# Attention probabilities of 16 heads turned in 32-blocks on VectorE and through a DRAM scratch, on one Trainium2 core

## The chip, the cores and the metric

One Trainium2 (trn2) chip, one core of it. The metric is the device time of one launch in microseconds (us). The profile's names: PE is TensorE (PEld its weight loads), DVE is VectorE, ACT is ScalarE, POOL is GpSimd, SP is SyncE; PEq, ACTq and so on are their sequencers. L979 is line 979 of the kernel before.

## The reference

Two blocks of two layers each on a sequence of 256 tokens, D = 1024, float32. The first: a short convolution mixer, then causal attention of 16 heads of 64 (as 256 keys are two of its blocks, each query sees its own block up to itself and all of the block before), each followed by a gated convolution FFN of 2816. The second: a pooling and state-space mixer, then a mixer of 8 heads with a forgetting bias (fox) and 8 latent heads (MLA, 96 wide), each followed by a gated FFN. What the change touches is this, for each head:

```python
sc = jnp.einsum('bhqd,bhkd->bhqk', qi, k).astype(F32) * scale
if fi is not None:
    sc = sc + fi[..., :, None] - log_decay_cum[:, :, None, :]
sc = jnp.where(kpos[None, :] <= qpos[:, None], sc, -jnp.inf)
p = jax.nn.softmax(sc, axis=-1).astype(v.dtype)
return jnp.einsum('bhqk,bhkd->bhqd', p, v)
```

## The kernel before

Everything stays in SBUF; only weights stream in, as 201 chunks of up to 1 MB (`PLAN`). SP loads a chunk into one of 4 raw buffers (`load`, L2153), ACT casts it to its high part (`hi`, L1223), DVE subtracts to get the low part (`lo`, L1570), and PE makes each product as three passes (high times high, high times low, low times high) of fp32r matmuls (`t_part`, L979, for products with tokens in rows; `f_block`, L901 to L923, for products with features in rows).

The order of work is written out by hand. `STEPS` is one list of steps for the whole kernel; each engine's program walks through it and does its own share of each step, in order, with semaphore waits (`Seq.wait_ge`). So a step's place matters only against the other steps of the same engine. The attention stages are the texts `MOBA` (heads 0 to 15) and `ODD` (heads 16 to 31: fox 16 to 23, MLA 24 to 31). In them:

- `tK.T` is a projection step: weight rows K, tokens T. `fN.B` is a step of the other form. `+h` and `+l` are one high cast (and, before, one load) and one low part.
- `sH`: PE makes the scores of heads H and H+1 (in `ODD` of H alone; `scores`, L1020); DVE scales, masks and takes the maxima (`maxima`, L1729); ACT takes the exponentials (`exps`, L1293 and L1295).
- `nH`: DVE multiplies by the reciprocal sum (`normalise`, L1737 to L1740).
- `uH`: PE turns the 128 x 384 probabilities of a head (tokens 0 to 127 against 128 keys, tokens 128 to 255 against 256 keys) in three 128 x 128 transposes into PSUM bank 6 (`turn_probs`, L1030), and ACT copies them out (`copy_probs`, L1302).
- `pH`: PE multiplies the values with the turned probabilities of up to four heads that end with H (`values`, L1048); ACT casts the result to its high part (`heads_hi`, L1306), DVE makes the low part (`split`, L1684).
- `ropeX.Q.T`: DVE rotates queries (Q = 1) or keys (Q = 0) of half X and tokens T (`rope_half`, L1748 to L1754). `crossX.Q.I`: PE turns them for the scores, waiting for both ropes of that half and kind (`cross`, L1058), and ACT copies them out (`copy_cross`, L1313 and L1315). The projection banks of a later stage are free only when the ropes of an earlier one are done (`t_bank_free`).
- In `ODD`, `qcopy` and `kcopy` (L1458, L1459) are ACT's copies of the fox queries and keys; `queriesT` is ACT's copy (L1433) and DVE's rope of the MLA queries; `acrossA.I` turns MLA queries and keys (L1156, copied at L1450) and waits for both `queries`; `kvsT` copies MLA keys and values. Turned probabilities, `cross` and `across` share PSUM bank 6.

A head's probabilities lie in one of four buffers (head number modulo 4), its turned ones in another four. The forget rows of the fox heads go through two small DMAs of SP (`fcrows`), in order with the weight loads.

## Time and profile before

| | us |
|---|---|
| median of 3 runs | 1202.39 (1202.03 to 1202.56) |
| the profiled execution | 1202.26 |
| its span, first to last instruction | 1201.0 |

Busy time in that span: PE 1192.8 us, DVE 880.8, ACT 660.9, POOL 52.6; the DMA engines move 217.8 MB. The granted TensorE clock is 0.999 of its full 2.4 GHz.

How to read it: a timeline row gives the start from the span's first instruction, the duration, engine, line, operation, what is written and read, the shape, and xN where N instructions are merged; in brackets stands the engine's idle time before it and what ended it. Matmuls are pipelined: the duration of one is longer than its distance to the next start, so a group's cost on PE is read from start to start. A `...q` row is the sequencer's, at which the engine itself may be idle.

### The profile page before, as it was taken

What the parts mean: (1) busy time and instruction counts of PE and PEld (TensorE: products, weight loads), DVE (VectorE), ACT (ScalarE), POOL (GpSimd) and SP (SyncE); (2) the same over time, 40 slices, a digit from 0 to 9 for tenths busy, and PEclk for the clock granted to TensorE, in tenths of its full rate; (3) what the DMA queues carried; (4) which work ended last, traced back from release to release, by engine and by line L of the source; (5) the groups of instructions that cost most, each with busy time, mean ns of one, the idle gap of its engine ahead of it and who ended that gap; (6) DMA issues with size and microseconds to landing.
All of it is one profiled execution on the core that took longest, in us unless ns stands there. A gap on an engine that the chain in (4) does not pass through costs nothing.

```text
span 1201.0 us, 16583 instructions
## 1 busy us (share of the span) xinstructions
PE 1192.8 (99%) x6629; PEld 1028.5 (86%) x6629; DVE 880.8 (73%) x1230; ACT 660.9 (55%) x871; POOL 52.6 (4%) x75
## 2 busy tenths in 40 slices
PE   9999999999999999999999999999999999999997
PEld 8888888888877888888899888888889977888886
DVE  6977989846786798883688877776467667777744
ACT  6555666634566666663587645444337775544430
POOL 0000000000000000000005200000002001000000
PEclk9999999999999999999999999999999999999999
DMA  9755555564534455556434556555526433755530
GB/s 357 249 207 192 170 183 188 189 223 162 204 109 141 190 179 177 206 196 218 158 106 141 181 211 240 189 197 188 183 91 229 176 140 106 251 204 176 193 123 35
DMA packets 32653, 217.81 MB, mean 181 GB/s; under 512 B 3760, under 2 KB 4032, under 8 KB 8000
## 3 DMA queue, kind: packets, MB, share of 16 engines
q1 hardware_dynamic: 30704, 210.39, 49.9%
q0 software_dynamic: 1728, 6.29, 1.6%
q8 instruction: 53, 0.87, 0.3%
q14 instruction: 24, 0.20, 0.0%
q10 hardware_dynamic: 144, 0.07, 0.0%
HBM read 215.67 MB, written 1.05 MB: 180 GB/s over the span
## 4 chain that ended last, share of the span: by engine, by line
PE 99%; DVE 0%; DMA 0%; ACT 0%; issue 0%
PE ps L979 43%; PE ps L901 24%; PE ps L907 14%; PE ps L909 4%; PE ps L923 2%; PE ps L920 2%; PE ps L919 2%; PE ps L1020 1%; PE ps L993 1%; PE ps L1048 1%; PE ps L1030 1%; PE ps L1112 1%; DMA t<-in_cst 0%; PE ps L1058 0%; PE ps L934 0%; PE ps L1097 0%
## 5 line engine op out<-in xcount | busy, mean ns | idle before, releaser
L979 PE MATMUL ps<-t,t 128*128 128x512 f32 (+4 forms) x2346 | 536.5, 385 | 0.0
L1570 DVE TENSOR_TENSOR t<-t,t 128x2048 fp32r<-128x2048 f32 (+3 forms) x200 | 448.7, 2256 | 101.4 <-PE ps L979 87.8
L979 PEld LDWEIGHTS ps<-t,t 128*128 128x128 f32 x2346 | 424.8, 188 | 81.4 <-issue 1.8
L1223 ACT CAST t<-t 128x2048 fp32r<-128x2048 f32 (+3 forms) x200 | 374.5, 1882 | 202.3 <-PE ps L979 105.6
L901 PE MATMUL ps<-t,t 128*128 128x512 f32 x1274 | 305.8, 390 | 0.0
L901 PEld LDWEIGHTS ps<-t,t 128*128 128x128 f32 x1274 | 238.9, 188 | 51.2
L907 PEld LDWEIGHTS ps<-t,t 128*128 128x128 f32 x1456 | 187.2, 191 | 7.4
L907 PE MATMUL ps<-t,t 128*128 128x256 f32 x1456 | 189.5, 283 | 0.0
L1719 DVE TENSOR_REDUCE t<-ps 128x512 f32<-128x1024 f32 x40 | 49.0, 1225 | 44.4 <-PE ps L909 44.4
L1672 DVE SCALAR_TENSOR_TENSOR t<-t,t,t 128x254 f32<-128x254 f32 (+1 forms) x176 | 73.2, 478 | 10.2 <-ACT t L1248 10.2
L1288 ACT CAST t<-t 128x512 fp32r<-128x512 f32 x44 | 27.2, 619 | 91.1 <-DVE t L1703 91.1
L1684 DVE TENSOR_TENSOR t<-t,t 128x512 fp32r<-128x512 f32 x48 | 33.2, 692 | 34.9 <-ACT t L1288 32.2
L909 PE MATMUL ps<-t,t 128*128 128x512 f32 x182 | 58.1, 397 | 0.0
L2055 POOL TENSOR_TENSOR t<-t,t 128x1 f32<-128x1 f32 x22 | 15.0, 681 | 935.4 <-DVE t L1625 522.5
L919 PE MATMUL ps<-t,t 128*128 128x256 f32 x192 | 49.0, 288 | 0.0
L920 PE MATMUL ps<-t,t 128*128 128x256 f32 x192 | 48.0, 283 | 0.0
L1284 ACT ACTIVATE t<-t 128x512 f32<-128x512 f32 x42 | 26.4, 628 | 29.2 <-DVE t L1672 29.2
L1248 ACT ACTIVATE t<-t,t 128x256 f32<-128x256 f32 x88 | 39.8, 500 | 1.4 <-DVE t L1999 1.4
L920 PEld LDWEIGHTS ps<-t,t 128*128 128x128 f32 x192 | 36.8, 191 | 0.5 <-issue 0.2
L919 PEld LDWEIGHTS ps<-t,t 128*128 128x128 f32 x192 | 36.7, 191 | 0.5 <-issue 0.2
L1504 ACT CAST t<-ps 128x512 fp32r<-128x512 f32 x28 | 15.6, 588 | 34.9 <-PE ps L993 34.8
L923 PE MATMUL ps<-t,t 128*128 128x256 f32 x192 | 30.9, 283 | 0.0
(224 smaller groups left out, 846.1 us busy)
## 6 DMA issues: line engine op xcount, KB each, us to landing
t<-in_wts SPq DMA_DIRECT2D x192, 1024.0 KB, 4.9
t<-in_rows POOLq DMA_DIRECT2D x12, 512.0 KB, 4.2
t<-in_wts SPq DMA_DIRECT2D x4, 528.0 KB, 4.0
t<-in_wts SPq DMA_DIRECT2D x2, 768.0 KB, 4.7
t<-in_wts SPq DMA_DIRECT2D x2, 592.0 KB, 3.8
t<-in_x_in SPq DMA_DIRECT2D x2, 512.0 KB, 4.2
out<-t SPq DMA_DIRECT2D x4, 256.0 KB, 2.2
t<-in_wts SPq DMA_DIRECT2D x2, 256.0 KB, 6.6
```

The source lines that it names most:

```text
L901: mm(ps[:, bank + m, :], H[:, kt, cols[m]], XT[:, kt, :, :].rearrange("p c s -> p (c s)"), start=kt == order[0], stop=False)
L907: mm(ps[:, bank + m, 0:S], L[:, kt, cols[m]], XTh[:, kt, :], start=False, stop=False)
L909: ins = mm(ps[:, bank + m, :], H[:, last, cols[m]], XT[:, last, :, :].rearrange("p c s -> p (c s)"), start=False, stop=True)
L919: mm(o, H[:, kt, c], XTh[:, kt, :], start=kt == 0, stop=False)
L920: mm(o, L[:, kt, c], XTh[:, kt, :], start=False, stop=False)
L923: ins = mm(o, H[:, kt, c], XTl[:, kt, :], start=False, stop=kt == 7)
L979: ins = mm(ps[:, bank, at:at + c1 - c0], a, w[:, k, c0:c1], start=first and part == 0, stop=kt == KTS[stage] - 1 and part == 2)
L1223: copy(wh[:, k, 0:w], wraw[:, r, 0:w]).then_inc(s_hi, 1)
L1248: activation(dst[:, sl], src[:, sl], ACT.Copy, scale=vcol(name, col + blk)).then_inc(done, 1)
L1570: tt(wl[:, k, 0:w], wraw[:, r, 0:w], wh[:, h, 0:w].bitcast(F32), ALU.subtract).then_inc(s_lo, 1)
L1672: ins = stt(out=o, in0=src[:, blk * S:(blk + 1) * S - n], scalar=vcol(name, col + blk + (taps - 1 - n) * stride), in1=o, op0=ALU.mult, op1 ...
L1719: nc.vector.reduce_sum(dst.rearrange("p (a s) -> p a s", a=2), halves, AX_X).then_inc(s_wide, 1)
```

## The change

The probabilities of heads 0 to 7 and 16 to 23 are no longer turned by PE. `dH` (DVE, `turn_squares`) transposes a normalised head in 32 x 32 squares into a buffer of its own. `wH` (ACT's queue, `spill_squares`) writes that buffer, 128 rows of 1536 bytes, to a DRAM scratch. `rH` (ACT's queue, `probs_back`) waits until it has landed, and reads it back in another order, 4 x 128 pieces of 384 bytes, into the head's turned buffer. The values step waits for that. Since the squares bring the keys of a 128-block into another order, the keys of those heads are stored in that order (copies out of PSUM at a stride of four elements), and they get a mask of their own, loaded once for each attention. The turned buffers of all heads are laid out as (a, c, i), four groups of 32 queries, so the values matmuls and the copy of a turned head take rearranged operands. Steps are moved about in `MOBA` and `ODD`, and SP's loads follow the steps `+l` instead of `+h`.

The core of the diff:

```diff
-t7.1
-@q1 t0.0 n1 t0.1 t1.0 +h t1.1 t2.0 +l +l vcopy0 t2.1 u0 s2 n2 u1 t3.0 t3.1 t4.0 n3 t4.1 t5.0 u2 s4 t5.1 u3 t6.0 t6.1
-n4 +h +l +h t7.0 t7.1
-@k1 t0.0 s6 n5 rope1.1.0 p3 t0.1 u4 t1.0 t1.1 t2.0 t2.1 t3.0 t3.1 u5 t4.0 n6 t4.1 t5.0 t5.1 +h +l u6 t6.0 t6.1 t7.0
-t7.1 cross1.1.0
-@v1 t0.0 t0.1 t1.0 n7 rope1.1.1 rope1.0.0 +h t1.1 rope1.0.1 u7 +l t2.0 t2.1 cross1.0.0 t3.0 +l t3.1 cross1.1.1 +h t4.0
+@q1 t0.0 n1 d1 w0 t0.1 t1.0 +h w1 t1.1 t2.0 r0 +l +l vcopy0 t2.1 s2 n2 r1 d2 t3.0 t3.1 w2 t4.0 n3 d3 t4.1 t5.0 s4 w3 r2
+t5.1 t6.0 t6.1 n4 d4 r3 +h +l +h t7.0 t7.1
+@k1 t0.0 s6 w4 n5 d5 rope1.1.0 t0.1 t1.0 t1.1 w5 t2.0 t2.1 t3.0 p3 r4 r5 t3.1 t4.0 n6 d6 t4.1 t5.0 w6 t5.1 +h +l r6 t6.0 t6.1
+t7.0 t7.1
+@v1 t0.0 rope1.1.1 t0.1 cross1.1.0 t1.0 n7 d7 rope1.0.0 +h w7 t1.1 rope1.0.1 +l t2.0 r7 t2.1 cross1.0.0 t3.0 +l t3.1 cross1.1.1 +h t4.0
...
-@vf kcopy0 lrms1.1 latent2 t0.0 t0.1 +h s16 n16 t1.0 t1.1 t2.0 t2.1 t3.0 krope t3.1 s17 t4.0 s18 n17 t4.1 t5.0 u16 s19
-+l +l +l t5.1 t6.0 +h +h vfcopy t6.1 n18 n19 t7.0 t7.1 f2.0 +l +h u17 f2.1 +l +h u18 qcopy1 f3.0 f3.1
-@uq kcopy1 u19 t0.0 s20 t1.0 s21 n20 t2.0 n21 +h s22 s23 queries0 t3.0 t0.1 p19 u20 n22 t1.1 t2.1 +h t3.1
-@ukv u21 t0.0 queries1 u22 +h n23 t1.0 p21 across0.0 kvs0 t0.1 across0.1 kvs1 t1.1 across0.2
-@odd_out t0.0 u23 +l +l +l t0.1 +h across0.3 t1.0 across1.0 t1.1 across1.1 s24 across1.3 +l t2.0 across1.2 n24 s25 s26
+@vf kcopy0 lrms1.1 latent2 t0.0 t0.1 +h s16 n16 d16 t1.0 w16 t1.1 t2.0 t2.1 t3.0 krope t3.1 s17 r16 t4.0 s18 n17 d17 t4.1 t5.0
+w17 s19 +l +l +l t5.1 t6.0 +h r17 +h vfcopy t6.1 n18 d18 n19 d19 t7.0 w18 t7.1 f2.0 +l +h w19 f2.1 r18 +l +h r19 qcopy1 f3.0 f3.1
+@uq kcopy1 t0.0 t1.0 s20 t2.0 s21 n20 d20 w20 n21 d21 +h s22 w21 s23 queries0 t3.0 t0.1 p19 r20 n22 d22 r21 t1.1 w22 t2.1 +h t3.1
+@ukv t0.0 queries1 +h n23 d23 w23 r22 t1.0 across0.0 kvs0 t0.1 p21 r23 across0.1 kvs1 t1.1 across0.2
+@odd_out t0.0 +l +l +l t0.1 +h across0.3 t1.0 across1.0 t1.1 across1.1 s24 across1.3 +l t2.0 across1.2 n24 s25 s26
...
-            pe.wait_ge(s_ptc, 16 * a + last + 1)
+            for i in range(first, last + 1):
+                way, n = probs_left(16 * a + i)
+                if way == "u":
+                    pe.wait_ge(s_ptc, n)
+                else:
+                    pe.wait_ge(*back(16 * a + i))
...
+                        o = ps[64 * (i % 2):64 * (i % 2) + 64, 7, n * S + q.start:n * S + q.stop]
+                        ins = mm(o.rearrange("p (c a i) -> p a c i", a=4, i=32), value_of(a, i, kt),
+                                 turned_probs(a, i)[:, :, c, :], start=kt == 0, stop=kt == 1)
...
+        def spill_squares(h):
+            n = D_AT[h]
+            act.wait_ge(s_square, n)
+            nc.scalar.dma_start(spill[n - 1], squares_of(h)).then_inc(s_spill[h % 4], 16)
+
+        def probs_back(h):
+            a, n = h // 16, D_AT[h]
+            act.wait_ge(*spilled(h))
+            if h % 16 >= 4:
+                act.wait_ge(s_pv, valued_at(h - 4))
+            nc.scalar.dma_start(ATT_MEM[a][1][:, h % 4, :].rearrange("p (a f) -> p a f", a=4),
+                                spill[n - 1].rearrange("q f -> (q f)").rearrange("(a p f) -> p a f", a=4, p=128)
+                                ).then_inc(s_back[h % 4], 16)
...
+                if is_k:
+                    for i in range(4):
+                        ins = copy(spread_keys(kh[0:64, 4 * m + i, :]),
+                                   in_spread_order(s3[64 * (i % 2):64 * (i % 2) + 64, i // 2, :]))
+                    ins.then_inc(s_kc, 1)
+                    return
...
-                dve.wait_ge(s_pt, H - 3)
+                way, n = probs_left(H - 4)
+                dve.wait_ge(*((s_pt, n) if way == "u" else (s_square, n)))
...
+        def turn_squares(a, h):
+
+            if squares_before(16 * a + h) is not None:
+                dve.wait_ge(*spilled(squares_before(16 * a + h)))
+            dve.wait_ge(s_pnorm, 16 * a + h + 1)
+            dst = squares_of(16 * a + h).rearrange("p (b c i) -> p c b i", b=4, c=3)
+            nc.vector.transpose(dst, ATT_MEM[a][0][:, h % 4, :].rearrange("p (c b i) -> p c b i", c=3, b=4)
+                                ).then_inc(s_square, 1)
...
-            if kind in ("pump", "pump_hi"):
+            if kind in ("pump", "pump_lo"):
                 load(nxt[0])
                 nxt[0] += 1
...
+            elif kind == "probs_mask":
+                sp.wait_ge(s_hl, 11 * k[0])
+                at = CST["spread_mask"]
+                dma((moba_mask if k[0] == 1 else odd_mask)[:], cst[:, at:at + 256]).then_inc(s_smask, 16)
```

## Rows read from the trace of the kernel before

**Rows 1.** The page: busy time of the engines, and the chain that ended last.
```profile
PE 1192.8 (99%) x6629; PEld 1028.5 (86%) x6629; DVE 880.8 (73%) x1230; ACT 660.9 (55%) x871; POOL 52.6 (4%) x75
...
PE 99%; DVE 0%; DMA 0%; ACT 0%; issue 0%
```

**Rows 2.** PE's waits: who waited for whom, total us, times, longest.
```profile
PE ps L1193 <- DVE t L1930: 1.2, 1, 1.2
```

**Rows 3.** Windows: length; busy us of PE, PEld, DVE, ACT, POOL; clock, DMA share.
```profile
303.00:386.00 83.00, 83.00 (x469) 64.06 (x468) 60.01 (x165) 49.93 (x110) 0.00 (x0) 1.00 0.40 142
...
922.00:1000.00 78.00, 77.80 (x487) 65.39 (x487) 51.03 (x170) 55.04 (x121) 1.13 (x2) 1.00 0.43 153
```

**Rows 4.** Timeline of PE: two turns of probabilities and what starts next.
```profile
324.22 0.49 PE L1030 MATMUL ps<-t,t 128*128 128x128 f32 x3
324.64 0.93 PE L1020 MATMUL ps<-t,t 64*128 64x128 f32 x8
...
342.79 0.49 PE L1030 MATMUL ps<-t,t 128*128 128x128 f32 x3
343.04 2.32 PE L979 MATMUL ps<-t,t 128*128 128x512 f32 x9
```

**Rows 5.** Timeline of ACT, first attention: the copy that follows exponentials 4 and 5.
```profile
333.13 0.46 ACT L1302 COPY t<-ps 128x384 f32<-128x384 f32 x1
```

**Rows 6.** Groups by line and form: busy us, mean ns of one.
```profile
L1740 DVE TENSOR_SCALAR t<-t,t 128x256 f32<-128x256 f32 x32 | 11.1, 348 | 0.0
```

**Rows 7.** Timeline of DVE, first attention.
```profile
340.10 0.68 DVE L1684 TENSOR_TENSOR t<-ps,t 128x512 fp32r<-128x512 f32 x1
...
341.35 2.28 DVE L1570 TENSOR_TENSOR t<-t,t 128x2048 fp32r<-128x2048 f32 x1
343.55 0.16 DVE L1737 RECIPROCAL t<-t 128x2 f32<-128x2 f32 x1
...
344.21 0.42 DVE L1748 TENSOR_TENSOR t<-ps,t 128x256 f32<-128x256 f32 x1
...
349.17 0.42 DVE L1748 TENSOR_TENSOR t<-ps,t 128x256 f32<-128x256 f32 x1 [2.75 <-PE ps L979]
```

**Rows 8.** Timeline of ACT at the start: its one DMA issue.
```profile
0.73 0.41 ACTq L1482 DMA_DIRECT2D t<-in_cst  x1
```

**Rows 9.** DMA issues: KB each, median us from issue to landing.
```profile
out<-t SPq DMA_DIRECT2D x4, 256.0 KB, 2.2
...
t<-in_cst ACTq DMA_DIRECT2D x1, 68.0 KB, 4.0
```

**Rows 10.** Timeline of PE, first attention: p3, projection steps, cross1.0.0.
```profile
336.10 1.52 PE L1048 MATMUL ps<-t,t 128*64 128x256 f32 x16
...
338.59 4.36 PE L979 MATMUL ps<-t,t 128*128 128x512 f32 x18
...
353.90 0.60 PE L1058 MATMUL ps<-t,t 128*128 128x128 f32 x4
```

**Rows 11.** Timeline of PE, second attention: s21, p19, steps of uq and ukv.
```profile
952.45 0.82 PE L1020 MATMUL ps<-t,t 66*128 66x128 f32 x4
...
957.69 1.52 PE L1048 MATMUL ps<-t,t 128*64 128x256 f32 x16
...
959.45 3.37 PE L979 MATMUL ps<-t,t 128*128 128x384 f32 x18
...
962.90 1.64 PE L979 MATMUL ps<-t,t 128*128 128x512 f32 x6
```

**Rows 12.** Timeline of DVE, second attention: maxima 21, ropes of queries1.
```profile
953.31 0.29 DVE L1729 CUSTOM_DVE_ANT_0 t<-ps,t 128x128 f32<-128x128 f32 x1 [1.07 <-PE ps L1020]
...
964.19 0.22 DVE L1748 TENSOR_TENSOR t<-ps,t 128x64 f32<-128x64 f32 x1 [1.84 <-ACT t L1433]
```

**Rows 13.** Timeline of ACT, second attention: a cast, and the copy of queries1.
```profile
960.83 1.91 ACT L1223 CAST t<-t 128x2048 fp32r<-128x2048 f32 x1 [0.60 <-PE ps L979]
...
963.56 0.59 ACT L1433 COPY t<-ps 128x512 f32<-128x512 f32 x1
```

More of the change, by code:

```diff
@@ L119 @@
 NCST = _n
+NFIX = CST["spread_mask"]
 def constants(gain):
@@ L322, in all_steps @@
     out += [("rows", 2)] + ffn_steps(0, 2)
-    out += [("rows", 3), ] + mixed_steps(MOBA, None, 3)
+    out += [("rows", 3), ("probs_mask", 1)] + mixed_steps(MOBA, None, 3)
     out += [("rows", 4)] + ffn_steps(1, 4)
@@ L366, with probs_left @@
 VALUED = [s[1] for s in STEPS if s[0] == "p"]
+U_AT = {s[1]: n for s, n in counted("u").items()}
+D_AT = {s[1]: n for s, n in counted("d").items()}
+SPREAD = set(range(8)) | set(range(16, 24))
+def probs_left(h):
+    return ("d", D_AT[h]) if h in D_AT else ("u", U_AT[h])
 def valued_from(last):
@@ L445, in program @@
     brow = fixed.take([128, 1024])
-    cs = fixed.take([128, NCST])
+    cs = fixed.take([128, NFIX])
     vecs = fixed.take([128, NVEC])
@@ L493, in program @@
     moba_mem = (area.take([128, 4, 384]), area.take([128, 4, 384]), area.take([128, 4, 8]))
+    moba_squares, moba_mask = area.take([128, 4, 384]), area.take([128, 256])
+    spill = nc.dram_tensor("spilled_probs", (len(D_AT), 128, 384), F32).ap()
     area = area_at(mix_base)
@@ L569, in program @@
     s_oh, s_ol = sem("s_heads_hi"), sem("s_heads_lo")
+    s_smask, s_square = sem("s_spread_mask_loaded"), sem("s_probs_squares_turned")
+    s_spill = [sem(f"s_probs{i}_spilled") for i in range(4)]
+    s_back = [sem(f"s_probs{i}_back") for i in range(4)]
     s_pw, s_us, s_xtap = sem("s_pool_w_loaded"), sem("s_u_copied"), sem("s_x_tap")
@@ L854, in qk_of, with squares_of, squares_before, turned_probs @@
         return (qmT if is_q else kmT)[:, h - 8, cols]
+    SPREAD_MASK = (moba_mask, odd_mask)
+    def squares_of(h):
+        if 16 <= h < 20:
+            return odd_squares[:, h % 2, :]
+        return (moba_squares if h < 16 else late_squares)[:, h % 4, :]
+    def squares_before(h):
+        return h - 2 if h in (18, 19) else h - 4 if 4 <= h < 16 else None
+    def turned_probs(a, h):
+        return ATT_MEM[a][1][:, h % 4, :].rearrange("p (a c i) -> p a c i", a=4, c=3)
+    def spilled(h):
+        return s_spill[h % 4], 16 * sum(d <= h and d % 4 == h % 4 for d in D_AT)
+    def back(h):
+        return s_back[h % 4], 16 * sum(d <= h and d % 4 == h % 4 for d in D_AT)
+    def in_spread_order(ap):
+        return ap.rearrange("p (n r b) -> p n b r", r=32, b=4)
+    def spread_keys(ap):
+        return ap.rearrange("p (n b r) -> p n b r", b=4, r=32)
     def att_scale(a, h):
@@ L1033, in values @@
         def values(a, last):
-            PT, first = ATT_MEM[a][1], valued_from(16 * a + last) - 16 * a
+            first = valued_from(16 * a + last) - 16 * a
             if first:
@@ L1440, in odd_step @@
                 act.wait_ge(s_t, T_AT["t", "ukv", 1, t])
+                for h in (18, 19):
+                    act.wait_ge(*spilled(h))
                 b2 = ps[:, 2 * t:2 * t + 2, :]
@@ L1449, in odd_step @@
                 act.wait_ge(s_acm, ACROSS_AT["across", a, i])
+                if a:
+                    for h in (22, 23):
+                        act.wait_ge(*spilled(h))
                 copy((kmT if a else qmT)[:, 2 * i:2 * i + 2, :].rearrange("p a b -> p (a b)"),
```

47 lines of the change are left out of this document (32 added, 15 removed).

## The prediction

> **What bounds the kernel now.** I read the page first. TensorE (PE) is busy for 99% of the span and the chain of work that ended last lies on it for 99% [rows 1]; the list of its waits for other engines holds three entries, and the longest, 1.2 us, is at the start [rows 2]. So a microsecond of matmul taken away in this kernel is a microsecond of time, as long as no other engine makes PE wait instead, and the question of the change is just that: PE gives work away, and VectorE (DVE), ScalarE (ACT) and the DMA engines must take it in without being late. Over the two attention stages, 303 to 386 us (call it the first attention) and 922 to 1000 us (the second), DVE is busy 60 of 83 and 51 of 78 us, ACT 50 and 55 [rows 3]; but those are sums, and what counts is where the free time lies. So I went on to the timelines of both stages, one engine at a time, and looked for two things: what PE pays for the turned probabilities, and how early DVE and ACT are with what PE asks next.
>
> **What is removed.** For 16 of the 32 heads the three transposes of a turn (`u`) go. The busy time of a group is 0.49 us, but matmuls overlap; what counts is from its start to the next start, 0.25 us among projection matmuls (343.04 - 342.79) and 0.42 beside scores (324.64 - 324.22) [rows 4]. Of the 16 groups that go (324.2 to 352.2 us and 932.6 to 972.5 us), ten take 0.24 to 0.25 and six 0.28 to 0.42; the sum is 4.5 us: 2.4 in the first attention, 2.1 in the second. With them go 16 copies of 0.46 us on ACT (L1302) [rows 5]. PE's values matmuls read and write the same counts in runs of 32 to 64 columns: I cost that at nothing, as no row has it either way; 0.1 us a head would be 3 us.
>
> **What is added, with its price.** (a) 16 DVE transposes of 128x384, which no row shows. A one-input DVE instruction of 256 columns takes 0.35 us [rows 6], which is 0.53 for 384 by its columns; a two-input one of 2048 columns takes 2.28 [rows 7], which is 0.43 for 384, and 0.86 if a transpose went at half the pace. I take 0.55, near the first row, and keep 0.4 to 0.9. (b) 32 DMA issues in ACT's queue: ACT's one issue in the trace holds its sequencer for 0.41 us [rows 8]. If a running activation hides it, it costs nothing; I take 0.35 (0 to 0.45). (c) Each way through DRAM: a 256 KB store lands 2.2 us after its issue, ACT's own 68 KB load in 4.0 us beside others [rows 9]. I take 2.4 us out and 2.8 back (2 to 4, and more for the way back, whose pieces are 384 bytes). (d) ACT waits, in order, for a head's squares to be turned (`w`), and for its spill to land before it reads it back (`r`). Queued behind are the weights' high casts, the exponentials and the copies that PE waits for. (e) The k copies read PSUM at a stride and the fox ones are four in place of two: 0.2 us each, ahead of s16 and s20. (f) SP's loads follow the low pumps instead of the high ones. SP waits for freed buffers anyway, and only its order against the forget rows changes, by one load. PE waits for weights nowhere [rows 2]. Nothing. The two masks are loaded far ahead: nothing.
>
> The Trainium skill's page "VectorE: DVE Perf Modes" (The three transpose paths) gives 311 ns for a 128x128 bf16 transpose on VectorE; three of them would be 0.93 us, an estimate from that page, against my 0.55, and would add some 1.5 us to the sum below (four of them on the paths that follow). No row here shows it. The Trainium skill's page "DMA: Bandwidth & Descriptors" (Anatomy of one DMA) says that about 2 us of each DMA are fixed, most of it the receipt of the write, and heaviest for HBM; that speaks against a wait on a spill. The 2.2 us store row agrees [rows 9].
>
> **The first attention, step by step.** Read-backs: ACT spills head 3 only after the exponentials of heads 4 and 5, which ended at 333.1 and now end near 332.2 [rows 5]; with an issue and 2.4 and 2.8 us its data are back near 338. PE reaches `p3` at 339.1: from 336.10, less 1.4 for four turns, plus six steps of 0.70 that now stand ahead of it and 0.2 about the scores [rows 10]. Just hidden. Then take the end of `p3` as zero. PE has 15 projection steps of 0.70 us (18 matmuls in 4.2 us) and one crossing turn of 0.36 until `cross1.0.0`: 10.9 us [rows 10]. For that turn DVE must have done both last ropes. From the same zero: ACT's cast 0.6, DVE's split 0.6, normalise 6 0.66, transpose 0.55, low weights 2.2, rope 2.2, normalise 7 0.66, transpose 0.55, and for two ropes and PE's start 4.75 (353.90 - 349.17): 12.8 us [rows 7, 10]. In the kernel before DVE stood idle for 2.75 us just ahead of those two ropes, waiting for PE [rows 7]: now PE comes 2.4 us earlier, `p3` stands six steps later, and DVE has transposes in between, so the cover is used up. PE waits 1.9 us. ACT also waits for spill 3, then casts two chunks and does four issues before it is free for the cast after `p3`, up to 0.9 us late: 2.7 us in all (1.5 to 3.5). Of the 2.4 us nothing is left.
>
> **The second attention.** Small waits first. `s20` needs `kcopy1`, now behind `w19`, `r18` and `r19` on ACT: 0.3 us. `s21`, `s22`, `s23` now follow each other, and `s23` needs the maxima of head 21, which start 0.86 us after `s21` (953.31 - 952.45) and take 0.56: 0.45 us [rows 11, 12]. So `p19` starts at 957.4, where it started at 957.69 [rows 11] although 1.06 us of transposes are gone. From there PE needs 1.45 for `p19`, 3.2 for three steps and 2.9 for two more, and stands before `across0.0` at 965.0 us [rows 11]. That needs `queries1`, and this is the place that decides. On ACT the order is `w20`, cast, exponentials 22, `w21`, exponentials 23, `queries0`, `w22`, cast, `queries1`. On DVE: maxima 21 done at 954.4 (as 953.31 to 953.87 before, half a microsecond later) [rows 12], normalise and transpose 20 1.2, so `w20` can issue at 955.6. Cast 1.8, twice 0.9 and two issues bring `queries0` to 960.0; its ropes end at 962.6 (0.6 and 2.0); split, normalise 22 and transpose 22 take 1.8: 964.4. Only now `w22` issues (0.35), the cast follows (1.8) and the copy of `queries1` starts at 966.6; 0.63 later its ropes start and take 2.0 [rows 12], so PE goes on at 969.4. Before, the same copy started at 963.56, with a cast from 960.83 ahead of it and nothing that waited for DVE [rows 13]. So PE waits 4.4 us (3.4 without the issues' cost, 4.8 with 0.45 each). Then `w23` and `r23` stand before the copies of `across0.0` and `across0.1`: 0.3 us.
>
> **The sum.** Removed 4.5. New waits 2.7 + 0.3 + 0.45 + 4.4 + 0.3 = 8.15. Net +3.6 us. The profiled execution took 1202.26 us (span 1201.0 and 1.3 around it), 0.1 below the median of the three runs; I forecast 1205.8 us. With both ends of the unknown costs the waits are 5.5 to 11, so 1203 to 1209.
>
> **The rivals.**
> - *All waits hidden* (faster): the heads' chains are loose enough, and the 4.5 us stay: 1197.9. For it: DVE and ACT have a third of these stretches free [rows 3]. Against it: the free time lies in the wrong places, and at the place that decides, `queries1` behind `w22` on ACT, the copy would have to start by 962.5 in place of 966.6. From that point on PE's wait there is nothing. Chance 0.14.
> - *Half hidden* (no change): issues cost nothing, transposes take 0.4, and ACT gets through `w22` earlier, so that the waits are 2 to 6 us: 1200 to 1204, say 1202.2. Chance 0.28.
> - *Landing late* (slower still): if the read-back goes at the pace of ACT's 68 KB load, 4.0 us for 68 KB [rows 9], its 192 KB need up to 11 us, and each values step waits for it. It decides from 4 us on, where `p3` would start late; at 7 us PE stands 4 us at `p3` and 2 more at `p7`: 1211. The Trainium skill's page "DMA: Bandwidth & Descriptors" (Why small descriptors are slow) states such a penalty for small pieces in HBM. Against it: the DMA engines are busy for only 0.40 and 0.43 of these stretches [rows 3]. Chance 0.12.
> - *Strided operands cost* on PE or in the k copies, so that the mechanism is neither wait: 3 us more, 1208. Chance 0.06.
>
> **How the numbers follow.** Forecast 0.40; its own range is 1203 to 1209. 0.2% (2.4 us) is about what a measurement of this kernel can tell from no change, so faster is below 1200.0 and slower above 1204.8. Faster: the first rival and a little of the second, 0.16. Same: most of the second and the low end of the forecast, 0.30. Slower: 0.54. The range leaves out the full gain and the worst landings: 1199.5 to 1210.5.
>
> **What would show it.** The profile after should have PE waiting for DVE's rope line at the crossing turn near 351 us for 1.5 to 3.5 us, and at the turn `across0.0` near 965 us for 3 to 5 us, with ACT idle ahead of `w22`; ACT's idle time released by DMAs in both stretches; DVE's transposes at 0.4 to 0.9 us. Those two waits under 1 us each would make the forecast wrong, and so would spill landings of over 4 us.

## The result and the profile after

The changed kernel takes 1213.37 us (median of 4 runs, 1212.64 to 1213.82) against 1202.22 us (1202.03 to 1202.56) of the kernel before in the same comparison: 1.0092 times as long, 95% interval 1.0079 to 1.0104. That is 11.1 us slower, where 3.6 us slower was forecast and 1210.5 us was the top of the range. Its profiled execution took 1213.82 us, with a span of 1212.5 us (before: 1201.0). In it e.g. L1071 is `scores` (L1020 before), L1105 `values`, L1115 `cross`, L1213 `across`, L1030 `t_part`, L1539 ScalarE's copies of the fox keys (`kcopy`), L1508 its copies of the MLA queries (`queries`), L1530 those of the turned ones (`across`), L1365 a spill, L1372 a read-back, L1843 VectorE's transpose of the squares, L1280 the high cast, L1858 the last instruction of a rope.

The page's busy times, and the shares of the chain that ended last, which answer to [rows 1]:

```profile
PE 1191.9 (98%) x6581; PEld 1024.3 (84%) x6581; DVE 889.7 (73%) x1246; ACT 655.5 (54%) x859; POOL 53.2 (4%) x75
...
PE 93%; DVE 3%; ACT 2%; DMA 1%; issue 0%; ACTq 0%; SPq 0%; DVEq 0%
```

And PE's waits, which answer to [rows 2] (who waited for whom, total us, times, longest):

```profile
PE ps L1071 <- ACT t L1539: 5.9, 1, 5.9
PE ps L1213 <- DVE t L1858: 4.1, 1, 4.1
PE ps L1115 <- DVE t L1858: 1.6, 1, 1.6
PE ps L1250 <- DVE t L2034: 1.2, 1, 1.2
...
PE ps L1071 <- DVE t L1824: 0.3, 1, 0.3
```

48 matmuls less, as 16 turns of three should give, and PE's busy time is nevertheless only 0.9 us less: part of its work ran slower. The 1.2 us are the start's, as before, and so is the row that is not shown (0.8 us at 6.9 us, for a weight chunk; 0.3 to 1.0 us at that place in the other kernels). The last row is the scores of head 19, at 932 us. The second and third rows are the two waits that the prediction put its sum on (4.4 and 2.7 us forecast, 4.1 and 1.6 found). The first row is the surprise: 5.9 us ahead of `s20`, where 0.3 was forecast. PE's timeline around it, and at `across0.0`:

```profile
956.10 1.62 PE L1071 MATMUL ps<-t,t 66*128 66x128 f32 x4 [5.87 <-ACT t L1539]
957.15 2.48 PE L1030 MATMUL ps<-t,t 128*128 128x384 f32 x6
...
976.50 0.61 PE L1213 MATMUL ps<-t,t 128*96 128x128 f32 x4 [4.13 <-DVE t L1858]
976.87 2.25 PE L1030 MATMUL ps<-t,t 128*128 128x512 f32 x6
```

In the kernel before the same six matmuls behind the scores took 1.42 us:

```profile
952.92 1.42 PE L979 MATMUL ps<-t,t 128*128 128x384 f32 x6
```

They take 2.48 here at 957.15, and six wider ones take 2.25 at 976.87 and 1.63 at 981.16. The windows (length; busy us of PE, PEld, DVE, ACT, POOL; granted clock, DMA share, GB/s) say why: the granted clock is at its lower level, 1.2 GHz, in two stretches in which PE has work.

```profile
953.80:960.50 6.70, 4.40 (x14) 4.16 (x15) 2.59 (x5) 3.07 (x10) 0.00 (x0) 0.50 0.50 168
960.60:977.60 17.00, 12.79 (x74) 10.39 (x74) 11.00 (x53) 9.92 (x18) 0.00 (x0) 1.00 0.18 58
977.70:981.00 3.30, 3.30 (x15) 1.83 (x14) 0.00 (x0) 1.61 (x4) 0.00 (x0) 0.50 0.40 118
```

What the engine did before it fell: in the first case PE stood idle and was still waiting as the clock fell, in the second it had just come out of 4.1 us of idleness. The stretches are 6.8 and 3.4 us long (953.74 to 960.57, 977.64 to 981.05), and PE works for 4.5 and 3.4 us of them. At half pace that costs 2.2 + 1.7 = 3.9 us. So the bill is 5.9 + 4.1 + 1.6 + 0.3 of waits, 3.9 of half clock, less the 4.5 us of turns: 11.3 us, against 11.5 between the two spans (1212.5 - 1201.0).

Why was ACT late with the copy at L1539? Its timeline and its queue's (ACTq):

```profile
942.51 0.34 ACTq L1365 DMA_DIRECT2D spilled_probs<-t  x1
942.89 1.91 ACT L1280 CAST t<-t 128x2048 fp32r<-128x2048 f32 x1 [2.96 <-DVE t L1843]
943.82 0.34 ACTq L1365 DMA_DIRECT2D spilled_probs<-t  x1
950.98 0.38 ACTq L1372 DMA_DIRECT2D t<-spilled_probs  x1
951.46 1.90 ACT L1280 CAST t<-t 128x2048 fp32r<-128x2048 f32 x1 [6.66 <-DMA spilled_probs<-t]
...
954.45 1.50 ACT L1539 COPY t<-ps 64x256 f32<-64x256 f32 x4
```

The spills of heads 18 and 19 go out at 942.51 and 943.82. The read-back `r18` waits for the first one to land, until 950.98, and behind it in ACT's order stand a cast, `r19`, `qcopy1` and `kcopy1`. The median landing over the whole execution is within the prediction's 2 to 4 us, though single ones are not: in the first attention some took up to 6.5 us, and PE waited for none of them. The DMA issues (KB each, median us from issue to landing), first those of the page, then of the window 962 to 975 us, then of 936 to 956 us:

```profile
spilled_probs<-t ACTq DMA_DIRECT2D x16, 192.0 KB, 3.1
t<-spilled_probs ACTq DMA_DIRECT2D x16, 192.0 KB, 2.9
```
```profile
spilled_probs<-t ACTq DMA_DIRECT2D x3, 192.0 KB, 1.8
```
```profile
t<-in_wts SPq DMA_DIRECT2D x5, 1024.0 KB, 6.5
...
spilled_probs<-t ACTq DMA_DIRECT2D x2, 192.0 KB, 7.9
```

A spill by itself lands in 1.8 us; these two took 8.5 and 7.4 us, and what is different is the company: three weight loads of 1 MB that SP issued at 937.5, 939.5 and 941.2 us and that landed at 943.5, 946.6 and 950.7. The windows 942 to 951 of after, and of before, where the loads ran without spills:

```profile
942.00:951.00 9.00, 8.23 (x64) 7.91 (x62) 3.94 (x6) 1.91 (x1) 0.00 (x0) 1.00 0.99 370
```
```profile
942.00:951.00 9.00, 9.00 (x74) 8.73 (x73) 3.95 (x2) 4.96 (x7) 0.00 (x0) 1.00 0.80 301
```

So the DMA engines were 0.80 busy in that place before the change put anything into it. Over the whole stages the windows, which answer to [rows 3], show little of it: PE busy for 1.6 and 10.4 us less than before, and a clock of 0.93 in the second.

```profile
303.00:386.00 83.00, 81.36 (x447) 61.66 (x446) 64.61 (x174) 48.27 (x102) 0.00 (x0) 1.00 0.54 183
...
922.00:1000.00 78.00, 67.44 (x381) 56.49 (x380) 46.52 (x145) 44.67 (x91) 0.00 (x0) 0.93 0.51 176
```

The experiments had to say whether the loads are the cause, whether ACT's place in it is, and what the half clock hangs on.

### The profile page after: what moved, and what is told of

Same layout as the page of the kernel before. It is cut to its first block, busy times and chain, and to the rows that moved or that the text cites. A ratio compares the mean times of both kernels' runs of the same rounds, so it can differ in the third digit from the quotient of the medians.

```text
span 1212.5 us, 16526 instructions
## 1 busy us (share of the span) xinstructions
PE 1191.9 (98%) x6581; PEld 1024.3 (84%) x6581; DVE 889.7 (73%) x1246; ACT 655.5 (54%) x859; POOL 53.2 (4%) x75
## 4 chain that ended last, share of the span: by engine, by line
PE 93%; DVE 3%; ACT 2%; DMA 1%; issue 0%; ACTq 0%; SPq 0%; DVEq 0%
PE ps L1030 40%; PE ps L952 24%; PE ps L958 14%; PE ps L960 4%; PE ps L974 2%; PE ps L971 2%; PE ps L970 2%; PE ps L1071 1%; PE ps L1044 1%; PE ps L1105 1%; DMA spilled_probs<-t 1%; ACT t L1280 1%; PE ps L1169 1%; PE ps L1081 1%; DMA t<-in_wts 0%
## 5 line engine op out<-in xcount | busy, mean ns | idle before, releaser
L1030 PE MATMUL ps<-t,t 128*128 128x512 f32 (+4 forms) x2346 | 536.4, 385 | 0.0
L1030 PEld LDWEIGHTS ps<-t,t 128*128 128x128 f32 x2346 | 426.1, 188 | 83.5 <-issue 2.7
L1280 ACT CAST t<-t 128x2048 fp32r<-128x2048 f32 (+3 forms) x200 | 374.5, 1883 | 218.8 <-PE ps L1030 102.5
```

Of the source, the lines that this page charges most:

```text
L1030: ins = mm(ps[:, bank, at:at + c1 - c0], a, w[:, k, c0:c1], start=first and part == 0, stop=kt == KTS[stage] - 1 and part == 2)
L1280: copy(wh[:, k, 0:w], wraw[:, r, 0:w]).then_inc(s_hi, 1)
```

## The experiments

Each group of four ran beside the kernel before on one chip; its median there was 1201.94, 1202.29, 1202.09 and 1202.00 us. Ratios are to it.

**Who is queued behind the late transfers.** First the two copies are taken out from behind ACT's waits, each by itself and then both.

```diff
-... w19 f2.1 r18 +l +h r19 qcopy1 f3.0 f3.1
-@uq kcopy1 t0.0
+... w19 f2.1 +l +h qcopy1 f3.0 f3.1
+@uq kcopy1 r18 r19 t0.0
```

> Only the read-backs of heads 18 and 19 are moved behind the second copy of the fox keys on ScalarE. Theory (that copy stood behind two read-backs which waited for spills of 8.45 and 7.45 us, and TensorE's clock fell after its 5.9 us of idle time): the wait at the scores of head 20 falls from 5.9 us to under 0.6, the granted clock of that stretch stays at 1.0, and the time falls by 5.9 us of waiting and up to 3.4 us of half clock, from 1213.4 to 1204 to 1208 us; the wait of 4.1 us at the first crossing turn of the MLA queries stays. Rival 1 (the strided copies of the keys, or DMA traffic itself, make the scores late): the wait stays above 4 us and the time near 1213. Rival 2 (the wait goes, but the values of heads 16 to 19 then wait for their late read-backs): 1209 to 1213, with TensorE waiting for a DMA at the values.

```diff
-... r21 t1.1 w22 t2.1 +h t3.1
-@ukv t0.0 queries1 +h n23
+... r21 t1.1 t2.1 +h t3.1
+@ukv t0.0 queries1 w22 +h n23
```

> Only the spill of head 22 is moved behind the copy of the second MLA queries on ScalarE. Theory (the prediction's step on this place: the copy stood behind a spill that waited for VectorE's transpose): the wait of 4.1 us at the first crossing turn falls to 0 to 1 us, the half clock behind it (3.4 us at half pace, so 1.7 us) goes, and the time falls by 4 to 6 us, to 1207.5 to 1209.5; the 5.9 us at the scores of head 20 stay. Rival (VectorE is the late one there, because its transposes and splits stand ahead of the ropes): the wait stays above 2.5 us, and the time falls by less than 3 us.

> Both moves at once: read-backs of heads 18 and 19 behind the second copy of the fox keys, spill of head 22 behind the copy of the second MLA queries. Theory (the two waits and the two stretches of half clock are the whole loss in the second attention, and they are independent): 1213.4 - 5.9 - 3.4 - 4.1 - 1.7 = 1198.3 if nothing is late next, 1199 to 1202 with small waits left. Rival (the costs are the work itself: the issues, the transposes, the strided operands of TensorE): 1205 or more.

Measured: 1206.91 us for the first (1.0045, 1.0029 to 1.0060), 1209.20 for the second (1.0065, 1.0048 to 1.0082), 1202.10 for both (1.0006, 0.9997 to 1.0015). PE's waits of the three, in this order:

```profile
PE ps L1105 <- DMA t<-spilled_probs: 2.5, 1, 2.5
PE ps L1115 <- DVE t L1858: 1.6, 1, 1.6
PE ps L1213 <- DVE t L1858: 1.4, 1, 1.4
```
```profile
PE ps L1071 <- ACT t L1539: 5.0, 1, 5.0
...
PE ps L1213 <- DVE t L1858: 1.1, 1, 1.1
```
```profile
PE ps L1105 <- DMA t<-spilled_probs: 3.0, 2, 1.8
```

Moving two DMA issues on ACT removes the 5.9 us, and moving one removes 3 of the 4.1; both theories hold, the strided copies are not to blame for the 5.9. But the late landing has not gone: it has found another waiter, the values (L1105), for 2.5 us, and 3.4 us of half clock came behind that wait as well. It also came ahead of the crossing turn, where the 4.1 us that were expected to stay shrank to 1.4. In the kernel with both moves the longest wait is 1.8 us and the clock stays up; its waits of 5.4 us in all use up the 4.5 that were removed, and the time is that of the kernel before. The 1.8 us are at `p3`, in the first attention, where nothing was changed: the read-back of head 3 took 6.4 us in this execution and 2.7 in that of the kernel after. Landings vary between executions of one order of steps, and part of the waits with them.

**Who issues.** All 32 transfers from SP's queue, or from GpSimd's, in the places of the kernel after.

```diff
-            act.wait_ge(s_square, n)
-            nc.scalar.dma_start(spill[n - 1], squares_of(h)).then_inc(s_spill[h % 4], 16)
+            sp.wait_ge(s_square, n)
+            nc.sync.dma_start(spill[n - 1], squares_of(h)).then_inc(s_spill[h % 4], 16)
```

> All 32 scratch transfers are issued by SyncE at the same steps, ScalarE issues none of them and waits for none of them; SyncE's weight loads are now queued behind their waits. Theory (what costs time is ScalarE standing at waits for transfers and for VectorE with TensorE's copies queued behind): both waits of the second attention, 5.9 and 4.1 us, and their half clock go, 1199 to 1202. Rival (the weight loads behind SyncE's waits come late, or the landing of the transfers itself is what TensorE waits for): TensorE waits at a projection step for a weight chunk or at the values for a read-back, 1204 or more.

> All 32 scratch transfers are issued by GpSimd, which has almost nothing to do in both stages; the weight loads are not queued behind its waits, and ScalarE is free of them. Theory: the waits of 5.9 and 4.1 us at the two copies go. The read-backs still land late where spills meet weight loads (7 to 8.5 us in all three kernels measured), so TensorE waits at the values of heads 16 to 19 for 1 to 4 us: 1201 to 1204. Against 1207.6 with SyncE as the issuer, where the loads were held behind the waits and the read-backs of head 18 and 19 were issued 2 to 4 us later. Rival (an issue of GpSimd costs more than one of SyncE or lands later): 1206 or more.

Measured: 1207.55 us with SP (1.0046, 1.0031 to 1.0061), 1203.21 with GpSimd (1.0013, 1.0000 to 1.0026; single runs from 1201.0 to 1208.6, the profiled one 1207.80). PE's waits, SP then GpSimd:

```profile
PE ps L1105 <- DMA t<-spilled_probs: 5.8, 2, 4.3
```
```profile
PE ps L1105 <- DMA t<-spilled_probs: 4.5, 2, 2.3
```

With either issuer the waits for the copies are gone, and the values wait for read-backs in their stead. With SP it is worse: its spills come right behind the loads in one queue, and took 5.8 us by the page's median (3.9 with GpSimd, 3.1 with ACT), and it issued the read-back of head 17 at 943.6 us, 7 us later than ACT had. For SP the rival was right, for GpSimd the theory, except that one of the two waits was at the values of heads 0 to 3.

**Are the loads the cause?** The kernel after, with two of the three loads of that burst held back until spill 19 has landed.

```diff
+            if i in (165, 166):
+                sp.wait_ge(*spilled(19))
             if i >= NRAW:
```

> The kernel after with one thing changed: two of the three weight loads that SyncE issued at 939.5 and 941.2 us, ahead of the spills of heads 18 and 19 (942.5 and 943.8), are issued only when the spill of head 19 has landed. Theory (those spills took 8.45 and 7.45 us because 1 MB loads were queued ahead of them): they land in under 3.5 us, the wait at the scores of head 20 falls from 5.9 us to under 1.5, its half clock goes, and the time is 1204 to 1208, if the two chunks, issued 5 to 6 us later, are still in time. Rival 1 (a spill in this place is slow by itself, by its 1536-byte pieces or as a write): they still take over 6 us and the wait stays. Rival 2 (the held chunks come late): TensorE waits at a projection step for a weight chunk, and the time is 1210 or more.

Measured: 1206.99 us (1.0043, 1.0028 to 1.0058). The DMA issues of its window 936 to 949 us, and its waits:

```profile
spilled_probs<-t ACTq DMA_DIRECT2D x2, 192.0 KB, 2.7
```
```profile
PE ps L1213 <- DVE t L1858: 3.4, 1, 3.4
...
PE ps L1105 <- DMA t<-spilled_probs: 1.0, 1, 1.0
PE ps L1071 <- ACT t L1539: 0.4, 1, 0.4
```

Nothing was moved but two loads, and the two spills land in 1.8 and 3.5 us in place of 8.5 and 7.4, and the 5.9 us at `s20` become 0.4. So the loads made the spills late. The held loads then ran together: the read-back of head 19, issued with them, took 10.5 us, and the spills of heads 20 and 21, at 955.5 and 957.3, took 6.1 and 4.8. The collision had only been moved on.

**What the rest of the change costs.** First everything of the change but the transposes and the trip: the order and the 32 turns of the kernel before, with the rearranged operands, the strided key copies, the masks and the loads after the low parts.

> The order of steps of the kernel before, with all 32 turns on TensorE and no scratch transfer, but with the other parts of the change: the turned buffers laid out in four groups of 32 queries, so rearranged operands of the values matmuls; the k copies at a stride, four in place of two; the spread masks and their loads; the weight loads following the low parts. The keys of 16 heads are in the spread order and their values are not, so the output differs from the reference. Theory (all of this costs nothing): 1202, within 0.1% of before. Rival (strided operands cost 0.1 us a head on TensorE, or the late loads leave a wait): 1204 to 1206.

Measured: 1202.46 us (1.0002, 0.9992 to 1.0011). These parts cost nothing that the time shows (0.2 us, and the interval is 1.2 us to either side). Its trace has one small wait of theirs, 0.3 us at `s20` for the strided copies of the fox keys (L1539). Then the transposes without the trip, in two versions:

```diff
-            if squares_before(16 * a + h) is not None:
-                dve.wait_ge(*spilled(squares_before(16 * a + h)))
-            dst = squares_of(16 * a + h).rearrange(...)
+            if h >= 4:
+                dve.wait_ge(s_pv, valued_at(16 * a + h - 4))
+            dst = ATT_MEM[a][1][:, h % 4, :].rearrange(...)
```

> The kernel after without the trip through DRAM: VectorE transposes the squares of a head straight into its turned buffer, TensorE's values wait for that transpose, and the 32 transfers with ScalarE's waits are left out (so the probabilities of 16 heads are only turned inside the squares, and the output differs from the reference). Theory (VectorE's transposes cost only the 1.6 us at the first crossing turn of the first attention; the rest of the loss is the trip and ScalarE's place in it): the waits of 5.9 and 4.1 us go, with the half clock, and the time is 1202.2 - 4.5 + 1.6 + some tenths, 1199 to 1200.5. Rival (the new order of the steps and VectorE's load make TensorE wait in the second attention too): 1203 or more, with a wait of over 3 us at a crossing turn there.

Measured: 1211.47 us (1.0074, 1.0058 to 1.0091), against both the theory and the rival's mechanism. The waits name a place that neither had:

```profile
PE ps L1030 <- DVE t L1840: 9.5, 4, 5.1
```

This is a wait that the experiment itself put in: a turned buffer is free only when the values of the head four before it are made, so VectorE stood at the transposes of heads 4 and 20, for 8.5 and 3.9 us, with the ropes queued behind, and PE's projections waited for the banks that ropes free. VectorE's timeline at head 4:

```profile
340.37 0.58 DVE L1825 STREAM_TRANSPOSE t<-t 128x384 f32<-128x384 f32 x1 [8.49 <-PE ps L1105]
```

Two stretches of half clock came with it, 3.9 us in the table below. The squares buffer of the change lets VectorE go on there, and that is worth 1211.5 - 1200.6 = 10.9 us, as the second version shows. It takes that wait away:

```diff
-            dst = squares_of(16 * a + h).rearrange(...)
+            dst = (squares_of(16 * a + h) if h >= 4 else ATT_MEM[a][1][:, h % 4, :]).rearrange(...)
```

> The trip through DRAM left out a second time, without the wait that spoiled the run before (there VectorE stood at transposes of heads 4 to 7 and 20 to 23 until the values of four heads earlier were made, with the ropes queued behind). Here VectorE transposes those eight into the squares buffer, waits for nothing of TensorE, and TensorE's values read what stands in the turned buffer; the 32 transfers and all waits for them are left out, so the output differs from the reference. Theory (the transposes on VectorE cost only the 1.6 us at the first crossing turn of the first attention): 1202.3 - 4.5 + 1.6 + some tenths = 1199 to 1200.5. Rival (VectorE's load costs more than that by itself): 1203 or more.

Measured: 1200.62 us (0.9987, 0.9978 to 0.9996).

```profile
PE ps L1115 <- DVE t L1838: 1.5, 1, 1.5
...
PE ps L1213 <- DVE t L1838: 1.0, 1, 1.0
```

So with VectorE's part alone, 4.5 us are removed and 3.0 us of waits are there, and the trip through DRAM, as the change makes it, costs 1213.4 - 1200.6 = 12.8 us.

**Is it the wait that brings the half clock?** The kernel before, with ACT's second `kcopy` made four times, or twice.

```diff
+                for _ in range(3 if is_k and m == 1 else 0):
+                    act.own(copy(d4[:, :, 0, :], s3[0:64]))
+                    act.own(copy(d4[:, :, 1, :], s3[64:128]))
+                    act.settle()
                 copy(d4[:, :, 0, :], s3[0:64])
```

> The kernel before, with nothing of the change: ScalarE makes the second copy of the fox keys four times in place of once, so that TensorE waits some 3.5 to 4 us ahead of the scores of head 20. Theory (a wait of this length brings a stretch of half clock, whatever made it): a stretch of 3.4 us at the lower clock right behind the wait, and 1202.3 + 3.7 + 1.7 = 1207 to 1208. Rival (the half clock belongs to the change): the clock stays, 1205.5 to 1206.5.

> The same with the copy made twice: TensorE waits 1.2 to 1.5 us. Theory: the clock stays at 1.0, and the time is 1202.3 + 1.3 = 1203.3 to 1203.8. Rival (any wait brings a stretch of half clock): 1205 or more.

Measured: 1207.84 us (1.0049, 1.0033 to 1.0064) and 1203.28 us (1.0009, 1.0000 to 1.0018). The wait and three windows of the first, then the wait and two windows of the second:

```profile
PE ps L1020 <- ACT t L1463: 3.6, 1, 3.6
```
```profile
950.00:955.50 5.50, 1.87 (x11) 1.53 (x10) 1.89 (x4) 4.29 (x8) 0.00 (x0) 1.00 0.57 198
955.60:958.90 3.30, 3.30 (x12) 3.12 (x11) 1.25 (x9) 1.50 (x7) 0.00 (x0) 0.50 0.04 15
959.00:962.00 3.00, 3.00 (x19) 2.90 (x19) 1.93 (x12) 3.00 (x8) 0.00 (x0) 1.00 0.00 0
```
```profile
PE ps L1020 <- ACT t L1463: 1.2, 1, 1.2
```
```profile
948.00:953.00 5.00, 3.80 (x27) 3.46 (x27) 2.37 (x2) 2.80 (x5) 0.00 (x0) 1.00 0.48 177
953.00:958.00 5.00, 5.00 (x31) 4.85 (x30) 3.46 (x21) 3.66 (x9) 0.00 (x0) 1.00 0.50 203
```

With nothing of the change in the kernel, a wait of 3.6 us brings 3.4 us at the lower level and one of 1.2 us brings none. In the traces of this case that were taken at full clock, no wait of up to 1.8 us had the lower level behind it, unless a longer one stood close by; those of 2.2 (two), 2.3, 2.5, 2.8, 3.3, 3.4, 3.6, 4.1, 4.3 and 5.0 us all had 3.4 us of it behind them, and those of 5.1 and 5.9 us had 6.8 us, part of it still idle. No wait between 1.8 and 2.2 us was seen. From 2.2 us on, a microsecond of waiting cost more than a microsecond.

**Versions that should win.** GpSimd issues, and three loads are held: one until the read-back of head 3 has landed, two until that of head 19. Then the same with head 7 moved behind the ropes in the first attention. The third has both of these and ACT as the issuer, with `w22` moved behind `queries1` (`r18` and `r19` stay ahead of `kcopy1`).

```diff
+            if i == 63:
+                sp.wait_ge(*back(3))
+            if i in (165, 166):
+                sp.wait_ge(*back(19))
```

> GpSimd issues the 32 scratch transfers, in the order of steps of the kernel after, and SyncE holds three weight loads until a read-back has landed: one until that of head 3, two until that of head 19. Theory (with GpSimd as issuer what is left of the loss are read-backs that meet weight loads, 4.5 us of waits at the values and a half clock behind them): TensorE waits at no values step for more than 0.3 us, the 1.6 us at the crossing turn stay, and the time is 1199 to 1200.5, with less spread than the 1201 to 1208.6 of the kernel without held loads. Rival (the late read-backs come from GpSimd's own issues, or other loads take the place of the held ones): waits of over 1 us at the values, 1202 or more.

> As the kernel before this one in the list, and in the first attention VectorE normalises and transposes head 7 after the two last ropes in place of ahead of them, the crossing turn stands one projection step later, and the values of heads 4 to 7 one step later. Theory (the 1.6 us there are VectorE's queue): the wait falls under 0.3 us, and the time is 1.4 us below the one without this, 1197.5 to 1199, which would be below the kernel before by 0.3%. Rival (the read-back of head 7, now about 1 us later, is what the values wait for): no gain, with a wait for a DMA near 360 us.

> ScalarE issues as in the kernel after. Three weight loads are held (until the read-backs of heads 3 and 19), the spill of head 22 stands behind the copy of the second MLA queries, and the ropes of the first attention stand ahead of head 7, as in the run above. Theory (where a transfer lands fast, it does not matter that ScalarE waits for it): the waits left are 0.4 us at the scores of head 20, 0.3 at those of head 23, about 1 at the crossing turn of the MLA queries and 0.5 at the copies behind it: 1202.3 - 4.5 + 2.2 + some tenths = 1200 to 1201.5. Rival (ScalarE's issues and waits cost more than GpSimd's in many small places): 1202 to 1204.

Measured: 1202.18 us (1.0000, 0.9991 to 1.0009), 1206.07 (1.0029, 1.0019 to 1.0039) and 1206.90 (1.0042, 1.0025 to 1.0059). The first has no wait at the values above 0.2 us, as expected, and its spread is 0.9 us in place of 7.6; but the time is 1.7 us above the top of the forecast, as it has three waits that the forecast did not count (1.1 at L1213, 0.7 in two for banks at L1030). The second is slower than the first by 4 us. Its profiled run was granted 0.56 of the clock from end to end (1980.14 us), so its waits can't be compared. Of its nine other runs two took 1202.1 and 1202.7 us at a granted clock of 0.999, and seven 1205.6 to 1208.0 at 0.996 or 0.997, where the first version had 0.998 or 0.999: so stretches of half clock are part of it. Which wait brings them is open; the rival named a values step that waits for head 7. The third is the case of the held loads again (its profiled run was the fastest of four, 1204.94 us). Its longest wait, and ACT's timeline ahead of it:

```profile
PE ps L1213 <- DVE t L1858: 3.3, 1, 3.3
```
```profile
961.92 0.94 ACTq L1372 DMA_DIRECT2D t<-spilled_probs  x2
962.95 1.91 ACT L1280 CAST t<-t 128x2048 fp32r<-128x2048 f32 x1 [3.14 <-DMA spilled_probs<-t]
...
964.76 0.58 ACT L1508 COPY t<-ps 128x512 f32<-128x512 f32 x1
```

The spills of heads 20 and 21 (7.2 and 5.8 us) now meet the loads that were held, ACT waits for them at `r20`, and the copy of `queries1` stands behind.

The last two change less and only where a trace showed a wait: the crossing turn two steps later in place of a new order on VectorE, and head 22 behind the MLA ropes. The version with GpSimd holds the three loads as before. The one with ACT holds only the load ahead of head 3's read-back, and has `r18` and `r19` behind `kcopy1`.

```diff
-... r7 t2.1 cross1.0.0 t3.0 +l t3.1 cross1.1.1 +h t4.0
+... r7 t2.1 t3.0 +l t3.1 cross1.0.0 t4.0 cross1.1.1 +h
-... t0.1 p19 r20 n22 d22 r21 t1.1 w22 t2.1 +h t3.1
-@ukv t0.0 queries1 +h n23
+... t0.1 t1.1 p19 r20 r21 t2.1 +h t3.1
+@ukv t0.0 queries1 n22 d22 w22 +h n23
```

> GpSimd issues, three weight loads held as before, and two changes of order: the first crossing turn of the last keys of the first attention stands two projection steps later, and in the second attention head 22 is normalised and transposed after the second MLA queries' ropes, with the values of heads 16 to 19 one step later. Theory: the 1.6 and 1.1 us of waits of the kernel with GpSimd and held loads (1202.2) go down to some 0.3 each: 1199.5 to 1200.5. Rival (something else is late next, as in the version that moved head 7 itself, which came out at 1202 to 1208): 1201.5 or more.

> ScalarE issues, the read-backs of heads 18 and 19 stand behind the second copy of the fox keys, the spill of head 22 behind the copy of the second MLA queries, the same two changes of order as in the kernel beside it, and only one weight load is held (until the read-back of head 3). Theory: of the waits of the kernel with both moves (1.8 at the values of heads 0 to 3, 1.6 at the crossing turn, 1.2 at the values of heads 16 to 19, 0.5 behind), 1 to 1.5 us are left: 1202.3 - 4.5 + 1.5 + 0.3 = 1198.5 to 1200, faster than both kernels. Rival (landings vary, and a values step waits over 2 us in some executions, with a half clock behind it): 1201 or more, with a spread of 3 us and more.

Measured: 1200.29 us with GpSimd (0.9982, 0.9973 to 0.9991) and 1202.23 with ACT (1.0003, 0.9994 to 1.0012). The first is 0.18% below the kernel before, the only full version whose interval lies below it; its forecast held. Its longest wait inside the two stages is one of 0.5 us, for a bank. The second missed its forecast (1198.5 to 1200); its runs go from 1201.3 to 1204.5 us, as its rival had it. Its trace has this (ACT's timeline, then PE's):

```profile
967.74 0.58 ACT L1530 COPY t<-ps 96x512 f32<-96x512 f32 x1 [0.92 <-DMA spilled_probs<-t]
```
```profile
968.37 0.76 PE L1213 MATMUL ps<-t,t 128*96 128x128 f32 x4 [2.19 <-ACT t L1530]
```

ACT's copy of `across0.0` stands behind `w23` and `r22`, PE waits 2.2 us, and the clock falls. With ACT as issuer the wait has now stood ahead of three copies in turn: that for `s20`, that of `queries1`, that of `across0.0`.

**The account.** For each profiled execution: PE's waits inside the two stages, half of PE's working time at the lower clock, and 4.5 us less where the turns are gone. The sum should be the difference of the spans to 1201.0 us. The kernel before has 0.2 us of such waits itself, which are not taken off.

| kernel | waits | half clock | sum with -4.5 | span's difference |
|---|---|---|---|---|
| after | 12.1 | 3.9 | 11.5 | 11.5 |
| e1_sync_issues | 7.9 | 1.7 | 5.1 | 5.6 |
| e2_pool_issues | 6.7 | 3.4 | 5.6 | 5.5 |
| e3_copies_first | 6.4 | 1.7 | 3.5 | 3.5 |
| e4_queries_first | 8.5 | 1.7 | 5.7 | 6.0 |
| e5_both | 5.4 | 0 | 0.9 | 0.9 |
| e7_no_trip | 9.9 | 3.9 | 9.3 | 9.3 |
| e8_loads_held | 6.9 | 1.7 | 4.1 | 4.3 |
| e9_squares_only | 3.0 | 0 | -1.5 | -1.5 |
| e10_pool_held | 4.1 | 0 | -0.4 | 0.2 |
| e12_act_held_all | 4.9 | 1.7 | 2.1 | 2.6 |
| e13_pool_reordered | 1.8 | 0 | -2.7 | -2.3 |
| e14_act_reordered | 3.3 | 1.7 | 0.5 | 0.7 |
| e15_before_late3 (turns kept) | 3.8 | 1.7 | (5.5) | 5.0 |

It closes within 0.6 us in 14 kernels (within 0.8 with the 0.2 us taken off and the waits outside the stages counted). e6 and e16, with the turns kept and no half clock, have 1.0 and 1.7 us of waits for 0.5 and 1.3 of span. So the 4.5 us of the turns were real, and within that accuracy waits and the clock took them back.

## Why the prediction was wrong

- *What is removed*, 4.5 us: right, by the account above and by the squares-only kernel.
- *(a) The transposes*: right. 16 of 0.58 us, half a microsecond from start to start, against 0.55 taken:

```profile
L1843 DVE STREAM_TRANSPOSE t<-t 128x384 f32<-128x384 f32 x16 | 9.3, 578 | 1.3 <-DVE t L1835 0.5
```

  The 0.93 us estimated from the Trainium skill's page "VectorE: DVE Perf Modes" (The three transpose paths) is not what this form takes (0.58); the measurement decides.
- *(b) The issues*: 0.34 us a spill and 0.37 a read-back, as taken, but mostly beside a running cast (943.82 in the timeline above), so they cost PE nothing that shows. *(e), (f)*, the strided copies and operands, the masks and the order of the loads: nothing in the time with the turns kept, and 0.3 us at `s20` in its trace, against 0.2 taken in (e).
- *The first attention*: the mechanism and the place were right, the size was off, 1.6 us against 2.7 (inside 1.5 to 3.5). The part over 1.9 us, ACT "up to 0.9 us late", did not come: its queue had room ahead of the crossing turn. `p3` was hidden in the profiled execution of the kernel after (PE came to it at 338.8 us, and head 3's data were back at 336.4); in that of the kernel with both moves, with the same order up to there, it waited 1.8 us. That it came out as hidden is in part luck.
- *The second attention*, `across0.0`: right, 4.1 against 4.4 us, for the reason given: ACT stands idle for 3.9 us ahead of the cast behind `w22`, until VectorE's transpose. (The terms as written add up to 969.2 us, so to 4.2.) How near it came is partly luck, as PE reached that place 7 us later than worked out, after the wait at `s20`; in the kernel with held loads, where the wait at `s20` was 0.4 us, this one was 3.4, with 1.0 at the values ahead of it. `s23`: 0.45 us forecast, under 0.1 found; its matmuls follow those of `s21` and `s22`, which ran at half clock in part. The 0.3 us of the list are at `s19`, a place that the prediction did not name.
- *The step that failed* is the first of the small waits: "`s20` needs `kcopy1`, now behind `w19`, `r18` and `r19` on ACT: 0.3 us". It counted the issues of `r18` and `r19` and not their wait, because (c) had the landing of a spill at 2.4 us and took 4 us for the worst. That price was near for a spill alone (1.8 us), and wrong by 6 us for one issued behind three weight loads. The prediction's own sign of being wrong, spill landings of over 4 us, came: 7 of the 16 took 4.2 to 8.5 us, and one of them made PE wait. The Trainium skill's page "DMA: Bandwidth & Descriptors" (Anatomy of one DMA) has about 2 us fixed for a DMA on GpSimd's path, before its bytes; spills alone took 2.1 us from GpSimd here and 1.8 from ACT, bytes included, so a little less than the page has. What could have been read from the kernel before is the DMA share of this place, 0.80 at 301 GB/s from 942 to 951 us; the prediction argued with 0.43, the mean of the whole stage [rows 3], the very error that it warned of in its first paragraph for DVE and ACT.
- *The rival "landing late"* was right in kind and had the chance 0.12. It priced the landing by bytes and looked for it at `p3` and `p7`; it was the company that made it late, and it struck at a copy that merely stood behind the wait. Its small pieces were no matter: read-backs in 384-byte pieces landed in 2.4 us where they ran alone (966.1 to 968.5 us).
- *A term that was missing*, put at nothing without a reason: the clock. 3.9 us of the 11.1 are matmuls at half pace behind two waits. Even with the right waits the sum lacked it: by what the other traces show, the forecast's own 4.4 us at `across0.0` would have brought 1.7 us more, and its 2.7 us at the crossing turn as much again.

With both corrected, the prediction's sum would be 3.6 + 5.6 for `s20` + 3.9 for the clock + 0.3 for `s19` - 1.1 - 0.3 - 0.45 - 0.3 for the crossing turn, `across0.0`, `s23` and the last small wait (`w23` and `r23`, which brought none), so 11.2 us, where 11.1 was measured.

## What to carry to other kernels

A transfer that something waits for is priced at the load of the DMA engines in the microseconds in which it is issued, not at its lone time or at the stage's mean share: 1.8 us became 8.5 behind three loads of 1 MB. A wait for a transfer belongs on a queue with nothing behind it that the bound engine needs; on ACT it moved from one copy to the next. And in a kernel with PE at 99%, a single wait of 2.2 us or more is to be priced with the matmuls at half clock behind it (1.7 us for each one from 2.2 to 5.0 us here), so that by these traces two waits of 1.8 us would cost less than one of 3.6.

## What had not been expected of the hardware

- A 192 KB spill issued 1.3 us behind the last of three 1 MB loads landed within 0.3 us of that load, 8.5 us after its issue (951.0 and 950.7 us). The Trainium skill's page "DMA: Bandwidth & Descriptors" (Queues, rings and completion order) says that each DMA engine takes turns between the queues it has work for, packet by packet. By that rule alone a spill would soon pass the loads that are queued on the other queue. In this trace it did so late: by the DMA view of these windows (q1 is SP's queue, q10 ACT's), 175 packets of SP's queue and none of ACT's ran from 942.5 to 946.0 us, 29 and 185 from 948 to 949 us, and the last five of the two spills ran after 950.5. The same section also says that the write that raises a DMA's semaphore lands only after every earlier write of that DMA engine, on any queue, which would hold a landing back. No run here tells what kept the first packets waiting for 3.5 us.
- The same kernel with GpSimd as issuer ran from 1201.0 to 1208.6 us. Its profiled run, 1207.8 us, has two waits of 2.2 and 2.3 us with 3.4 us of half clock behind each; the two slowest of its ten runs had a granted clock of 0.997, the others 0.998 to 1.0. So part of the spread is that a landing decides whether a wait is short enough for the clock to stay up; the rest is not traced.
- GpSimd's issues occupied it for 0.55 us (a spill) and 0.75 us (a read-back), and its spills landed alone in 2.1 us, against 1.8 from ACT. On an engine with nothing else to do that was the cheapest place.
